# Retrieved experts on a reduced token set: dense products for the prompt tokens, per-token gathering for the sampled tokens, and another order in sampled attention

## The reference

```python
def peer_ffn(x, wq, subkeys, u_tab, v_tab):      # x: 288 tokens x 2048
    q = (xf @ wq).astype(f32).reshape(n, PEER_HEADS, 2, PEER_HALF)
    s = jnp.einsum('nhpd,hpkd->nhpk', q, subkeys.astype(f32))
    top_s, top_i = lax.top_k(s, PEER_TOPK)                 # 16 of 128 keys, twice
    ...
    best_s, best_j = lax.top_k(cand_s, PEER_TOPK)          # 16 of 256 pairs
    expert = jnp.take_along_axis(cand_i, best_j, axis=-1)  # 0 .. 16383
    gate = jax.nn.softmax(best_s, axis=-1)
    ...
        h = gelu(einsum('nd,nhkd->nhk', xb, u_tab[eb]))    # 8 heads x 16 experts
        return einsum('nhk,nhkd->nd', gb * h, v_tab[eb])
```

## Time and profile before

| | us |
|---|---|
| median of 3 runs | 3494.63 (3493.28 to 3498.08) |
| the profiled execution | 3492.92 |
| its span, first to last instruction | 3491.3 |
| mean granted clock of TensorE, share of full speed | 0.906 |

### The profile page before, as it was taken

The page is one execution under the profiler, slowest core; times in us unless marked ns, Lnnn a source line. Parts: engine busy times, 40 slices in busy tenths (PEclk is TensorE's granted clock), DMA queues, the critical chain, the costliest instruction groups (busy, mean ns, idle before and its releaser), DMA issues. The chain is left out here.

```text
span 3491.3 us, 51890 instructions
## 1 busy us (share of the span) xinstructions
PE 3091.8 (89%) x21404; PEld 2822.5 (81%) x21404; DVE 1866.0 (53%) x3305; ACT 1029.7 (29%) x1188; POOL 108.3 (3%) x204
## 2 busy tenths in 40 slices
PE   3999749999965884696999999999999999999996
PEld 3999628888731332495999999999999999999995
DVE  3444256666666641245899888544444444444444
ACT  2222211111121110123444433333334433333332
POOL 0000000000031001000000000000000000000000
PEclk7999859898975567798999999999999999999998
DMA  2444200000035015232444444544445654445441
GB/s 118 156 156 157 101 6 10 20 10 20 10 100 201 2 49 193 91 129 105 163 165 160 156 165 158 171 165 162 169 163 198 209 185 166 165 162 169 162 165 64
DMA packets 106340, 442.90 MB, mean 127 GB/s; under 512 B 22729, under 2 KB 42930, under 8 KB 62738
## 3 DMA queue, kind: packets, MB, share of 16 engines
q1 hardware_dynamic: 93202, 400.11, 33.5%
q0 software_dynamic: 12928, 39.86, 3.4%
HBM read 422.24 MB, written 17.58 MB: 126 GB/s over the span
## 5 line engine op out<-in xcount | busy, mean ns | idle before, releaser
L2142 DVE TENSOR_TENSOR px_w_r<-px_w,px_wh 128x2048 fp32r<-128x2048 f32 x272 | 623.9, 2294 | 724.3 <-ACT px_wh L1978 723.6
L1978 ACT ACTIVATE px_wh<-px_w 128x2048 fp32r<-128x2048 f32 x272 | 521.5, 1917 | 1098.0 <-PE px_bank L256 601.0
L254 PE MATMUL px_bank<-pe_high,px_wh 128*128 128x288 f32 x2304 | 686.2, 298 | 25.6 <-DVE px_w_r L2142 25.6
L255 PE MATMUL px_bank<-pe_low,px_wh 128*128 128x288 f32 x2304 | 680.4, 295 | 0.0
L256 PE MATMUL px_bank<-pe_high,px_w_r 128*128 128x288 f32 x2304 | 677.9, 294 | 0.0
L254 PEld LDWEIGHTS px_bank<-pe_high,px_wh 128*128 128x128 f32 x2304 | 432.7, 188 | 26.0 <-issue 26.0
L256 PEld LDWEIGHTS px_bank<-pe_high,px_w_r 128*128 128x128 f32 x2304 | 434.7, 189 | 0.0
L255 PEld LDWEIGHTS px_bank<-pe_low,px_wh 128*128 128x128 f32 x2304 | 433.4, 188 | 0.0
L254 PE MATMUL px_bank<-px_arena_gh,px_wh 128*128 128x288 f32 x1024 | 303.3, 296 | 1.1 <-ACT px_h L2015 1.1
L254 PE MATMUL px_pair<-px_arena_gh,px_wh 128*128 128x288 f32 x1024 | 303.1, 296 | 0.0
L255 PE MATMUL px_pair<-px_arena_gl,px_wh 128*128 128x288 f32 x1024 | 302.1, 295 | 0.0
(11 more groups left out here) (426 smaller groups left out, 4832.7 us busy)
## 6 DMA issues: line engine op xcount, KB each, us to landing
px_w<-in_peer_u SPq DMA_DIRECT2D x128, 1024.0 KB, 4.9
px_w<-in_peer_v SPq DMA_DIRECT2D x128, 1024.0 KB, 4.8
in_w<-in_w_in SPq DMA_DIRECT2D x49, 1024.0 KB, 4.8
out_w<-in_w_o SPq DMA_DIRECT2D x16, 1024.0 KB, 4.8
px_w<-in_peer_wq SPq DMA_DIRECT2D x16, 1024.0 KB, 4.8
pq_pages<-in_kv_pages SPq DMA_DIRECT2D x48, 256.0 KB, 6.8
pq_pages<-in_kv_pages POOLq DMA_DIRECT2D x48, 256.0 KB, 5.8
g_rest<-px_rest POOLq DMA_DIRECT2D x36, 256.0 KB, 2.6
```

The source lines that it names most:

```text
L254: pe.matmul(out, w_high, high, start=start, stop=False, skip_group_check=True)
L255: pe.matmul(out, w_high, low, start=False, stop=False, skip_group_check=True)
L1978: act.activation(w_high[t % 2][:], w[t % SL][:], ACT.Copy).then_inc(raised, 1)
L2142: v.tensor_tensor(w_low[t % SL][:], w[t % SL][:], w_high[t % 2][:], ALU.subtract) \
```

## The change

1. **Dense products over 256 tokens.** The u and v tiles multiply the 256 prompt tokens only (ND = 256 in place of NY = 288). The 16 query tiles, the selection and the scores still have 288. The placing steps are 32 in place of 36. A v pass holds two blocks of outputs in one bank, so each of the two output halves (dh) has four banks of its own.
2. **Sampled tokens, u side.** TensorE transposes the 32 sampled tokens' activations to rows (rounds 1 to 4, four transposes each), and GpSimd stores them in DRAM. VectorE lists the 128 experts of each token as row numbers (list_experts, ahead of the first placing step). During the 64 v tiles of half 0, for each token and each half of 1024 inputs, GpSimd issues two transfers of 512 KB: the token's own half row to all 128 partitions, and an indirect one that brings 128 half rows of u. VectorE multiplies them (times_x), ScalarE sums along the row (sum_products). One step goes with each v tile, with two buffers.
3. **Sampled tokens, v side.** During the 64 u tiles of half 1, every second tile, an indirect transfer brings a token's 128 rows of v (1 MB), and TensorE multiplies them in float32 by a column matrix that is zero except for this token's column (own_values: four products of 32 stationary and 512 moving columns). At the start of half 1's v tiles the sums are transposed back and added to the residual.
4. **The v table in DRAM** keeps the order of the reference, so that rows can be gathered; a dense v tile is then read in pieces of 4 KB in place of 8 KB.
5. **Sampled attention.** TensorE's order is turn_pair(i), values(i), scores(i+1), give_back(i), and VectorE divides (divide) ahead of taking the next pair's largest.

The core of the diff:

```diff
                     finish(i)
+                    divide(i)
                     if i + 1 < PAIRS:
                         largest(i + 1)
                     give(i)
...
                     turn_pair(i)
+                    values(i)
                     if i + 1 < PAIRS:
                         scores(i + 1)
-                    values(i)
                     give_back(i)
...
-STEPS = NY // G8
+ND = NY - TS
+STEPS = ND // G8
...
+                pool.wait_ge(x_taken, 4)
+                pool.dma_start(x_rows, xrows).then_inc(x_stored, 16)
...
+                pool.wait_ge(x_stored, 16)
+                pool.wait_ge(listed, 3)
+                pool.wait_ge(placed, STEPS)
+                for n in range(2 * TS):
+                    if n >= 2:
+                        pool.wait_ge(u_summed, n - 1)
+                    part_ = x_rows[n // 2:n // 2 + 1, n % 2 * HALF:n % 2 * HALF + HALF]
+                    pool.dma_start(u_x[n % 2], bass.AP(part_.tensor, part_.offset, [[0, P], [1, HALF]])) \
+                        .then_inc(u_in[n % 2], 16)
+                    pool.indirect_dma_start(u_row[n % 2], None, halves, bass.IndirectOffsetOnAxis(
+                        ids[:, 1 + n % 2, n // 2:n // 2 + 1], 0)).then_inc(u_in[n % 2], 16)
+
...
+                def fetch_values(j):
+                    if j < 2:
+                        pool.wait_ge(u_summed, 2 * TS)
+                    else:
+                        pool.wait_ge(v_used, j - 1)
+                    pool.indirect_dma_start(v_row[j % 2], None, a["peer_v"], bass.IndirectOffsetOnAxis(
+                        ids[:, 0, j:j + 1], 0)).then_inc(v_in[j % 2], 16)
...
+                    if k >= 3 and k % 2:
+                        fetch_values((k - 3) // 2)
+                for j in range((STEPS - 2) // 2, TS):
+                    fetch_values(j)
...
+                def sum_products(n):
+                    act.wait_ge(u_timed, n + 1)
+                    act.activation(u_row[n % 2], u_row[n % 2], ACT.Copy,
+                                   accum_out=acts[:, n // 2, n % 2:n % 2 + 1]).then_inc(u_summed, 1)
...
+                    if 0 <= t - 1 - v_zero < 2 * TS:
+                        sum_products(t - 1 - v_zero)
...
+                    n = NY if tiles[t][0] == "q" else ND
...
-                        mm = split_product(pe, bank[t % SL][:, 0:NY], w_high[t % 2][:, k * P:k * P + P],
-                                           w_low[t % SL][:, k * P:k * P + P], high[:, k, :], low[:, k, :],
+                        mm = split_product(pe, bank[t % SL][:, 0:n], w_high[t % 2][:, k * P:k * P + P],
+                                           w_low[t % SL][:, k * P:k * P + P], high[:, k, 0:n], low[:, k, 0:n],
...
+                        out = bank[4 * dh + b][:, d % 2 * ND:d % 2 * ND + ND]
...
+                def turn_rows(r):
+                    if r:
+                        pe.wait_ge(x_taken, r)
+                    for c in range(4):
+                        mm = pe.transpose(bank[7][0:TS, c * P:c * P + P], xT[:, 4 * r + c, ND:NY], ident[:])
+                    mm.then_inc(x_turned, 1)
+
+                def own_values(j):
+                    if j == 0:
+                        pe.wait_ge(drained, 16)
+                    pe.wait_ge(v_ready, j + 1)
+                    pe.wait_ge(v_in[j % 2], 16 * (j // 2 + 1))
+                    for g in range(4):
+                        mm = pe.matmul(bank[7][TS * g:TS * g + TS, :], column[j % 2][:], v_row[j % 2][:, 512 * g:512 * g + 512],
+                                       start=j == 0, stop=j == TS - 1, skip_group_check=True)
+                    mm.then_inc(v_used, 1)
...
+                    j, odd = divmod(t - u_one - FIRST_V, 2)
+                    if 0 <= j < TS and not odd:
+                        own_values(j)
+                    if t == v_one + 6:
+                        turn_back()
...
+                def list_experts():
+
+                    lk(v.scalar_tensor_tensor(idf[:], picks[:, 0, ND:NY], float(NK), picks[:, 1, ND:NY], ALU.mult, ALU.add))
+                    v.tensor_copy(ids[:, 0, :], idf[:]).then_inc(listed, 1)
+                    lk(v.tensor_scalar(own[:], idf[:], 2.0, None, ALU.mult))
+                    v.tensor_copy(ids[:, 1, :], own[:]).then_inc(listed, 1)
+                    lk(v.tensor_scalar(idf[:], own[:], 1.0, None, ALU.add))
+                    v.tensor_copy(ids[:, 2, :], idf[:]).then_inc(listed, 1)
+                    v.wait_ge(listed, 3)
...
+                def times_x(n):
+                    v.wait_ge(u_in[n % 2], 32 * (n // 2 + 1))
+                    v.tensor_tensor(u_row[n % 2], u_row[n % 2], u_x[n % 2], ALU.mult).then_inc(u_timed, 1)
...
+                def own_column(j):
+                    if j >= 2:
+                        v.wait_ge(v_used, j - 1)
+                    v.tensor_scalar(column[j % 2][:], iota[:, 0:TS], float(j), own[:, j:j + 1], ALU.is_equal,
+                                    ALU.mult).then_inc(v_ready, 1)
...
+                    if 1 <= t <= 4:
+                        take_rows(t - 1)
+                    if 0 <= t - v_zero < 2 * TS:
+                        times_x(t - v_zero)
```

More of the change, by code:

```diff
@@ L1600, in finish, with divide @@
                             .then_inc(s_moved_v, 1)
-                def give(i):
+                def divide(i):
                     stat_ = s_stat[:, i % 2]
@@ L1860, in peer_experts @@
         iota = sb("iota", [P, NK])
-        h = [sb(f"h{s}", [P, NY]) for s in range(2)]
+        h = [sb(f"h{s}", [P, ND]) for s in range(2)]
+        ids = sb("ids", [P, 3, TS], U32)
+        idf = sb("idf", [P, TS])
+        acts = sb("acts", [P, TS, 2])
+        own = sb("own", [P, TS])
+        column = [sb(f"column{k}", [P, TS]) for k in range(2)]
+        rows_at = -(-nc.sbuf_base // 32) * 32
+        sb("rows", [P, D])
+        lay = Arena(nc, "px_lay", rows_at, D * 4)
+        xrows = lay("xrows", [TS, D])
+        lay.used = 0
+        u_row, u_x = [lay("u_row0", [P, HALF])], [lay("u_x0", [P, HALF])]
+        lay.used = 0
+        v_row = [lay("v_row0", [P, D])]
+        lay.used = 0
+        y_rows = lay("y_rows", [P, 512])
         rest = [sb(f"rest{s}", [P, EH, G8]) for s in range(3)]
@@ L2055, in _ @@
                         spread_gates(hf, k)
+                    if 0 <= t - 1 - v_zero < 2 * TS:
+                        sum_products(t - 1 - v_zero)
+                    if t == u_one + 2:
+                        act.wait_ge(u_joined, 1)
+                        act.activation(own[:], own[:], ACT.Gelu).then_inc(u_curved, 1)
+                    if t == v_one + 5:
+                        act.wait_ge(v_used, TS)
+                        act.activation(y_rows, bank[7][:], ACT.Copy).then_inc(y_kept, 1)
             @block.tensor
@@ L2120, in place, with turn_back @@
                     mm.then_inc(placed, 1)
+                def turn_rows(r):
[13 more added lines that the diff above has]
+                    mm.then_inc(v_used, 1)
+                def turn_back():
+                    pe.wait_ge(y_kept, 1)
+                    for c in range(4):
+                        mm = pe.transpose(bank[6][:, c * P:c * P + P], y_rows[:, c * P:c * P + P], ident[:])
+                    mm.then_inc(y_turned, 1)
                 pe.wait_ge(x_low, 4)
@@ L2336, in _ @@
                         take_picks()
+                        list_experts()
                     for hf, k in after[t + 1] if t + 1 < NT else ():
@@ L2343, in _ @@
                             lower_gates(t + 2)
+                    if 1 <= t <= 4:
+                        take_rows(t - 1)
+                    if 0 <= t - v_zero < 2 * TS:
+                        times_x(t - v_zero)
+                    if t == u_one + 1:
+                        join_halves()
+                    if t == u_one + 3:
+                        spread_own()
+                    j, odd = divmod(t + 1 - u_one - FIRST_V, 2)
+                    if 0 <= j < TS and not odd:
+                        own_column(j)
+                    if t == v_one + 7:
+                        add_own()
                     if t < PER_HEAD * PH + 5:
```

90 lines of the change are left out of this document (64 added, 26 removed).

## The result

The changed kernel takes 3362.51 us in the median (3359.41 to 3367.29), against 3493.95 of the kernel before, run beside it: a ratio of 0.962, with a 95% interval of 0.961 to 0.964. The forecast was 3338, its range 3315 to 3440. The profiled execution lasted 3360.29 us, its span 3358.6 us. So the span is 132.7 us shorter, where the steps of the prediction add up to 156.6.

What follows compares the result with a forecast made beforehand. Columns on TensorE, busy 89% of the span, were taken to set the time, not transfers. Terms from -163.8 (dense products) to +29.1 (values) sum to -156.6: 3492.9 becomes 3336.3, plus 1.7 for the median, 3338 us; range 3315 to 3440.

Steps and rivals of the forecast that it cites:

- Dense products, -163.8: Expert stretch: 256 u and v tiles at 256 columns, a product taking 120.0 ns in place of 133.3, -163.8 us.
- Rival C: Dense products: weight loads, not columns, hold a product at 133 ns, so -163.8 goes and time is 3502; chance 0.03.
- The u gather, +5: First v pass: two 512 KB transfers a tile fit narrowly, 6.5 us alone and up to 9.1 under load; +5 us.
- the slack, 9.4 us: First v pass: a gather may last about 9.4 us from its buffer's release before TensorE stands still.
- rival A: First v pass: the gather paces the tiles; at 12 us a tile takes 7.05, total 3416; at 9.4 nothing; chance 0.30.
- the signs named: First v pass: ScalarE's tile starts 5.76 to 6.0 us apart, or 6.5 and more if rival A holds.
- The shared port, 0.05 of rival A: Indirect issues blocked up to 2.3 us each by VectorE's two-input operations, 63 us at most, 3338 to 3396; chance 0.05.
- The limit of the memory: Gather tiles: the skill's 358 GB/s would need 5.86 us a tile, sum 1 to 2 us worse; trace moved 396 GB/s.
- Sampled attention, -25.6: New order removes two page waits (-41.2 us) and exposes three softmax waits of 5.22 us: -25.6, bounds 18 to 33.
- The steps of the values, +29.1: TensorE: 32 steps of four products in overlapping column groups, 0.91 us a set, +29.1 us.
- Selection and placing: Selection heads just fit, no loss taken, bound 0.5 us a head (4 us); 32 placing steps in place of 36, -7.1 us.

Runs made afterwards that it cites:

- vector_sums: Changed kernel with multiply and sum in one VectorE operation in place of ScalarE's sum, same transfers: 3324.3 us, ratio 0.952.
- no_u_gather: Changed kernel with both u-side transfers sent only for the first two steps, multiplies and sums still run: 3326.06 us, ratio 0.9525.
- experiment 5: vector_sums with GpSimd's refill also waiting for VectorE's next remainder (3377.47 us) or ScalarE's next rounding (3326.29 us); its table compares release times across five kernels.
- held_issue: vector_sums with one wait added, GpSimd refilling a buffer only after ScalarE's next rounding: 3326.29 us, ratio 0.9515.

## Why the prediction was right or wrong

The direction was right and the time within the range, but 24 us above the forecast. By its own steps, on the spans of the profiled executions:

**Dense products, -163.8: right in mechanism, a little more came.** v tiles take 5.76 us to the digit. u tiles take less: without a step of the values beside it one lasts 5.65 us, 117.7 ns a product, as these two starts of roundings show:

```profile
2553.63 1.92 ACT L2040 ACTIVATE px_wh<-px_w 128x2048 fp32r<-128x2048 f32 x1 [2.90 <-PE px_bank L256]
2559.28 1.92 ACT L2040 ACTIVATE px_wh<-px_w 128x2048 fp32r<-128x2048 f32 x1 [2.79 <-PE px_bank L256]
```

Over 128 u tiles that is 14 us more than forecast. Why a u product is 2.3 ns shorter than a v product at 256 columns, while both took 133.3 ns at 288, wasn't tried. Rival C is ruled out for this change, as v products start 120.0 ns apart.

**The u gather, +5: this step failed.** In the pass it cost 401.1 - 369.1 = 32 us, and 4.6 more at its end, where the last multiplies still stand in VectorE's queue ahead of remainders (the interval after the rounding of tile 146 is 10.27 us, against 5.76 in `vector_sums`). Together 36.6, and `no_u_gather` is 36.5 us below the changed kernel in the median (35.4 in the span). The prediction worked out the slack, 9.4 us, and that was right: the release came 3.77 us after the rounding's start, where it had 3.7, and the table of experiment 5 shows the loss begin where landings pass the slack. It then took 6.5 us for the gather alone and 9.1 at most. The trace shows 0.85 us to the second issue and 8.5 to the landing in the median, 9.35, and 11.3 us for the slowest landing:

```profile
L2006 POOL DMA_INDIRECT px_lay_u_row<-in_peer_u_rows,px_ids x32: 979/1328/2503, 2121.8 to 2524.9; - x32
...
DMA to landing us min/median/max: 5.3/8.5/11.3
```

So the median gather just reaches the limit, and any that is slower than the median stops TensorE. Two errors made the term: the upper bound took the dense load's share as the only thing that could slow it, and the sum used a typical value where the loss is made by the spread. (Its 2.2 us of fixed delay doesn't come out of the earlier trace rows either: 2.9 less 0.54 of issue and 0.66 for the data leaves 1.7, so the rows would have given an even shorter gather.) That was rival A, at 0.30, whose mechanism the runs show; its price for a mean gather of 9.4 was "nothing". A had every tile stretched alike, and the signs named were 5.76 to 6.0 us a tile without A and 6.5 or more with it; the mean of 6.27 is neither, being made of 27 long tiles and 37 of about 5.76.

**The shared port, 0.05 of rival A: the hold is real and small.** An indirect issue takes 0.98 us in the open. In the changed kernel the one at 2251.22 starts while VectorE's remainder of the gates runs, which has two SBUF inputs, and lasts 1.33 us; in `held_issue` an issue lasts 1.80 behind the weights' remainder. The longest, 2.50, started with 1.65 us of such an operation left. Each ends 0.85 us after that operation. "SBUF — State Buffer" of the Trainium skill, on the shared port, says that the two block one another; the trace agrees for the side of GpSimd alone. VectorE isn't held: its 64 remainders in the pass last 2282 to 2294 ns, and the one at 2306.45 of `vector_sums` starts at its usual 1.95 us after ScalarE's rounding and lasts 2.29, while the issue of 2305.88 is still running. My worry was 2.3 us on each; it was 0.35 in the usual case. What it adds to the 36.6 us isn't separated by a run: `held_issue` shows 0.8 us of it costing nothing with enough slack, and with the slack of the changed kernel 0.35 us would count, as the step from 3.25 to 3.77 in the table counts.

**The limit of the memory.** "DMA: Bandwidth & Descriptors" of the Trainium skill, under Specifications, has about 358 GB/s a core, as one of two cores' shares of a stack, and the prediction said that a tile would then need 5.86 us; this kernel runs on one core. The pass of `vector_sums` moved 358 GB/s, but at 5.76 us a tile with no stall, so it moved what was asked for, and no run here shows that as a ceiling.

**Sampled attention, -25.6: right in mechanism, mis-sized; 36.2 came.** The two waits of 20 us for pages are gone, and three waits of 5 us for the exponential are new, as forecast (-41.2 + 14.9 = -26.3; the first row below answers to the first of the earlier trace rows):

```profile
1292.65 3.87 PE L1754 MATMUL pp_pair<-ident,as_prob 128*128 128x128 f32 x16 [5.22 <-ACT as_prob L1648]
...
1325.25 3.58 PE L1754 MATMUL pp_pair<-ident,as_prob 128*128 128x128 f32 x16 [4.97 <-ACT as_prob L1648]
...
1355.71 3.71 PE L1754 MATMUL pp_pair<-ident,as_prob 128*128 128x128 f32 x16 [4.97 <-ACT as_prob L1648]
...
1386.30 3.77 PE L1754 MATMUL pp_pair<-ident,as_prob 128*128 128x128 f32 x16 [4.97 <-ACT as_prob L1648]
```

The windows that hold the same 564 products, of before and of after, show the rest:

```profile
1270.00:1450.00 180.00, 109.47 (x564) 49.01 (x564) 28.53 (x95) 16.19 (x29) 21.21 (x40) 0.76 0.37 130
```

```profile
1270.00:1415.00 145.00, 104.77 (x564) 53.40 (x564) 29.44 (x101) 16.83 (x30) 21.53 (x40) 0.83 0.46 162
```

TensorE stands 70.5 us in the first and 40.2 in the second, 30.3 less, which is 4 more than the named waits (small waits such as the 2.07 us between transposes went with the old order); and it is busy 4.7 us less at a granted clock of 0.83 in place of 0.76. The clock moved in one direction only, where I had let it cancel.

**The steps of the values, +29.1: mis-sized, about 41.** The set lasts 0.99 us, near the 0.91 taken from the earlier trace rows, and the column groups overlap as assumed. But a step stops a stream of products and starts it again: the rows below show two u tiles with one step take 12.59 us (5.71 and 6.88), 1.29 more than two of 5.65. The term left out the 0.3 us around each set, 9.6 us in all, and had the sets 2.6 us too small together.

```profile
2703.36 1.91 ACT L2040 ACTIVATE px_wh<-px_w 128x2048 fp32r<-128x2048 f32 x1 [4.29 <-PE px_bank L256]
2709.07 1.91 ACT L2040 ACTIVATE px_wh<-px_w 128x2048 fp32r<-128x2048 f32 x1 [3.12 <-PE px_bank L256]
2715.95 1.91 ACT L2040 ACTIVATE px_wh<-px_w 128x2048 fp32r<-128x2048 f32 x1 [4.30 <-PE px_bank L256]
```

**Selection and placing.** -44.3 came for these tiles. With u tiles of 5.65 us the steps would give 7 us more than the -42.5 forecast, so some 5 were lost; the heads of the selection, where VectorE had "nothing to spare", last 36.7 to 37.3 us in the main, and the first placing steps have a wait or two. After the first head (37.9 us) one lasts 36.75 us and six last 37.2 and more, some 3 us together, within the bound of 0.5 us a head; where the rest went wasn't looked for.

The five misses add up: +31.6 (gather), +12 (values), -14 (u products), -10.6 (attention), +5 (selection) = +24, which is 156.6 - 132.7. Of the 49 us that were left out, half were offset by errors of the other sign, so the total looks better than its terms.

## What to carry to other kernels

A transfer that is waited for in the queue of an engine that also feeds TensorE must be costed as a loop: from the release of its buffer to its use, against the slowest landing under load, not the median. Before more buffers or fewer bytes, look at what releases the buffer; here a sum folded into the multiply freed it 3.2 us sooner and gave back all that the gather had cost, 38 us of the time, with the same bytes at a DMA share of 0.97. And a set of products put between others costs its own time and the stop and start around it.

## What the runs showed of the hardware that was not expected

- An operation that multiplies and also sums along the row takes VectorE 1.22 us for 1024 elements (and 0.08 us to read the sum), as long as the multiply alone (1.225 us); ScalarE's sum took 1.05 us and 0.19.
- An indirect issue of 128 rows takes GpSimd 0.98 us, 0.54 for a direct one, and ends 0.85 us after a two-input operation of VectorE that was running when it began.
- One product of 32 stationary and 512 moving columns in float32 takes as long as four in four column groups, 0.98 against 0.99 us.
- A product in the rounded format takes 133.3 ns with 288 columns, 120.0 (v tiles) or 117.7 (u tiles) with 256, and 111.7 with 224: below 256 a column saved is worth less.
